# Mixture stage in units of 896 columns, four light experts, one set of PSUM banks

## The reference

```python
logits = x @ w_router;  top_vals, top_idx = top_k(logits, 2);  gates = softmax(top_vals)
for e in range(8):      # combine[e] = gate of e for the tokens that chose e, else 0
    out += combine[e] * ((silu(x @ we_gate[e]) * (x @ we_up[e])) @ we_down[e])
```

## Time and profile before

| | before |
|---|---|
| median of 3 runs, us | 1305.75 |
| profiled execution: its own time, us | 1306.28 |
| profiled execution: span from first to last instruction, us | 1304.5 |
| TensorE matmul busy | 1258.1 us, 96% |
| VectorE busy | 1115.2 us, 85% |
| ScalarE busy | 930.0 us, 71% |
| read from memory | 428.66 MB |
| DMA busy in the 40 slices of the page | 4 to 9 tenths in slices 0 to 11, 9 in slices 12 to 38 |

### The profile page before, as it was taken

How to read it: one execution, slowest core, us unless ns; L and a number is a source line. 1 busy time by engine, 2 the same in 40 slices (tenths; PEclk the granted TensorE clock), 3 DMA queues, 4 the chain that set the end, 5 groups by cost and what they waited for, 6 DMA issues and landing times.

```text
span 1304.5 us, 15757 instructions
## 1 busy us (share of the span) xinstructions
PE 1258.1 (96%) x6233; PEld 1052.4 (81%) x6233; DVE 1115.2 (85%) x873; ACT 930.0 (71%) x734; POOL 47.7 (4%) x57
## 2 busy tenths in 40 slices
PE   9999999999999999999999999999999999999986
PEld 8988888888888888777877887787777788777875
DVE  6987555577989999899899899988999999989897
ACT  5675444454877887888787777878878887878763
POOL 0100000001000000000000000000000000000110
PEclk9999999999999999999999999999999999999998
DMA  9948555546569999999999999999999999999992
GB/s 319 345 144 271 187 190 191 193 139 217 189 222 346 397 398 389 399 397 397 398 397 401 397 400 386 397 398 397 398 401 397 397 397 397 395 397 397 402 397 77
DMA packets 190147, 435.52 MB, mean 334 GB/s; under 512 B 8196, under 2 KB 50228, under 8 KB 175732
## 3 DMA queue, kind: packets, MB, share of 16 engines
q1 hardware_dynamic: 186272, 421.06, 86.5%
q0 software_dynamic: 3712, 13.37, 2.9%
q10 hardware_dynamic: 84, 0.02, 0.0%
HBM read 428.66 MB, written 5.77 MB: 333 GB/s over the span
## 4 chain that ended last, share of the span: by engine, by line
PE 40%; DMA 38%; DVE 13%; ACT 7%; issue 2%; SPq 0%; DVEq 0%; ACTq 0%
DMA raw<-in_we_down 29%; DVE w_lo L978 11%; ACT w_hi L619 7%; DMA raw<-in_we_up 6%; PE turn L1736 4%; PE turn L1733 4%; PE accp L1624 4%; PE accp L1626 4%; PE accp L1625 4%; PE turn L1624 3%; PE turn L1626 3%; PE turn L1625 3%; DMA raw<-in_we_gate 2%; PE turn L1735 2%; PE turn L1734 2%
## 5 line engine op out<-in xcount | busy, mean ns | idle before, releaser
L978 DVE TENSOR_TENSOR w_lo<-raw,w_hi 128x2048 fp32r<-128x2048 f32 (+1 forms) x401 | 905.5, 2267 | 114.9 <-ACT w_hi L619 110.4
L619 ACT CAST w_hi<-raw 128x2048 fp32r<-128x2048 f32 x395 | 755.1, 1914 | 214.8 <-DMA raw<-in_we_up 73.4
L1624 PE MATMUL turn<-w_hi,a_hi 128*128 128x512 f32 x552 | 218.8, 396 | 4.8 <-DVE w_lo L978 4.8
L1626 PE MATMUL turn<-w_hi,a_lo 128*128 128x512 f32 x552 | 215.4, 390 | 0.0
L1625 PE MATMUL turn<-w_lo,a_hi 128*128 128x512 f32 x552 | 215.0, 389 | 0.0
L1991 PE MATMUL turn<-w_hi,t_both 128*128 128x512 f32 x336 | 134.8, 401 | 6.9 <-DVE w_lo L978 6.6
L1992 PE MATMUL turn<-w_lo,t_both 128*128 128x512 f32 x336 | 131.5, 391 | 0.0
L1624 PE MATMUL accp<-w_hi,hT_hi 128*128 128x512 f32 (+1 forms) x284 | 113.0, 398 | 16.0 <-DVE hT_lo L978 16.0
L1624 PEld LDWEIGHTS turn<-w_hi,a_hi 128*128 128x128 f32 x552 | 103.8, 188 | 27.3 <-DVE w_lo L978 6.4
L1626 PEld LDWEIGHTS turn<-w_hi,a_lo 128*128 128x128 f32 x552 | 103.6, 188 | 22.1
L1625 PEld LDWEIGHTS turn<-w_lo,a_hi 128*128 128x128 f32 x552 | 103.8, 188 | 20.5
(11 more groups left out here) (287 smaller groups left out, 1566.5 us busy)
## 6 DMA issues: line engine op xcount, KB each, us to landing
raw<-in_we_gate SPq DMA_DIRECT2D x112, 1024.0 KB, 11.3
raw<-in_we_up SPq DMA_DIRECT2D x112, 1024.0 KB, 11.5
raw<-in_we_down SPq DMA_DIRECT2D x112, 1024.0 KB, 11.4
raw<-in_w_in SPq DMA_DIRECT2D x18, 1024.0 KB, 8.8
raw<-in_w_down SPq DMA_DIRECT2D x11, 1024.0 KB, 5.0
raw<-in_w_gate SPq DMA_DIRECT2D x10, 1024.0 KB, 5.3
raw<-in_w_up SPq DMA_DIRECT2D x10, 1024.0 KB, 5.2
raw<-in_w_out SPq DMA_DIRECT2D x8, 1024.0 KB, 9.4
```

What stands on the lines that cost most here:

```text
L619: nc.scalar.copy(w_hi[:, p % PARTS, :], raw[:, p % RING, :]).then_inc(hi_done, 1)
L978: return nc.vector.tensor_tensor(out, whole, hi.bitcast(f32), ALU.subtract)
L1624: nc.tensor.matmul(to, lh, rh, start=start, stop=False, **group)
L1626: return nc.tensor.matmul(to, ll, rh, start=False, stop=stop, **group)
```

## The change

An expert is cut into 4 units of 896 columns (`WIDE`) instead of 7 steps of 512. A unit has twelve pieces instead of six: four of gate and four of up (2 blocks of rows x 896 columns, 1792 of the 2048 columns of a slot, one run being 896 x 4 = 3584 bytes) and four of down (three with two rows per partition, 8192 bytes a run, and one with a single row, 4096 bytes a run). Gate and up sums of 896 columns lie as 2 x 448 in two banks each, and there is only one set: gate in the first two banks of `turn`, up in the other two. h of the unit before is turned into the gate banks, after the first of the four pieces of up (`amid_up`). Four experts instead of three are light, and the last expert is the fourth light one, whose four units end the order. `VISITS`, `SUM_AT` and the lists of ScalarE and VectorE are moved to fit. The first gate runs its hi x hi pass over all rows first.

```diff
-    N_STEPS = E * STEPS
     E_PIECES = 6 * STEPS
-    LIGHTS = 3
+    QUARTERS = 4
+    WIDE = FF_E // QUARTERS
+    PART = WIDE // 2
+    BLOCKS = WIDE // P
+    N_UNITS = E * QUARTERS
+    U_PIECES = 12
...
-    LIGHTS = 3
+    LIGHTS = 4
...
-    ORDER = "HHH" + "HLHLHHL" * 6 + "HLHLHLH" + "HHHH"
-    assert ORDER.count("H") == HEAVIES * STEPS and ORDER.count("L") == LIGHTS * STEPS
+    ORDER = "HHH" + "LH" * 12 + "H" + "L" * QUARTERS
...
+    FETCHED = (("L", 0), ("H", 1), ("L", 1), ("H", 2), ("L", 2), ("H", 3), LAST_ONE)
+    VISITS = ((1, 0), (3, 1), (8, 2), (10, 3), (13, 4), (16, 5), (20, 6))
...
+    SUM_AT = (1, 2, 4, 6)
+    PICK_AT = 7
...
-        return MOE_AT + (6 * i - 2 if i else 0)
+        return MOE_AT + (U_PIECES * i - 4 if i else 0)
...
+    def blocks_of(half):
+        return range(2 * half, min(2 * half + 2, BLOCKS))
+
+    def filled(p):
+
+        q = p - MOE_AT
+        if q < 0:
+            return PIECE
+        at = q + U_PIECES - MOE_PIECES if q >= MOE_PIECES - 4 else (q - 8) % U_PIECES if q >= 8 else q
+        return 2 * WIDE if at < 8 else len(blocks_of(at - 8)) * D
...
-        def gate_bank(i):
-            return turn[:, 2 * (i % 2), :]
-
-        def up_bank(i):
-            return turn[:, 2 * (i % 2) + 1, :]
+        gate_banks, up_banks = (turn[:, 2 * i:2 * i + 2, 0:PART] for i in range(2))
+        hT_bank = turn[:, 0:2, :].rearrange("p b c -> p (b c)")[:, 0:WIDE]
+        gateT_bank, upT_bank = turn[:, 0, 0:PART], turn[:, 1, 0:PART]
+        sums_bank = turn[:, 1, PART:PART + 4]
+        tokens_bank = turn[:, 2:4, :].rearrange("p b c -> p (b c)")
+        picks_bank = turn[:, 2, 0:TOK]
...
-                dst = raw[:, p % RING, :].rearrange("p (k f) -> p k f", k=src.shape[1])
+                dst = raw[:, p % RING, 0:filled(p)].rearrange("p (k f) -> p k f", k=src.shape[1])
                 sp.dma_start(dst, src).then_inc(slot_filled[p % RING], 16)
...
+                        for pair in range(4):
+                            load(step_at(i) + 4 * j + pair,
+                                 expert_rows(w, ORDER[i], k)[:, 2 * pair:2 * pair + 2, s * WIDE:(s + 1) * WIDE])
                 if i:
                     k, s = expert_step(i - 1)
-                    for half in range(2):
-                        r0 = (2 * s + half) * HALF
-                        load(step_down(i - 1) + half, expert_part(we_down, ORDER[i - 1], k, r0))
+                    for pair in range(4):
+                        r0 = (BLOCKS * s + 2 * pair) * P
+                        load(step_down(i - 1) + pair, expert_part(we_down, ORDER[i - 1], k, r0, len(blocks_of(pair))))
...
             def leave_gate(i):
-                used(step_at(i) + 1)
+                used(step_at(i) + 3)
                 if light(i):
-                    nc.scalar.copy(silu_e[:, i % 2, :], gate_bank(i)).then_inc(few_copied, 1)
+                    nc.scalar.copy(parts(silu_e[:, i % 2, :]), gate_banks).then_inc(few_copied, 1)
                 else:
-                    nc.scalar.activation(silu_e[:, i % 2, :], gate_bank(i), ACT.Silu).then_inc(e_silu, 1)
+                    nc.scalar.activation(parts(silu_e[:, i % 2, :]), gate_banks, ACT.Silu).then_inc(e_silu, 1)
 
             def leave_up(i):
-                used(step_at(i) + 3)
-                nc.scalar.copy(h_e[:, i % 2, :], up_bank(i)).then_inc(few_copied, 1)
+                used(step_at(i) + 7)
+                nc.scalar.copy(parts(h_e[:]), up_banks).then_inc(few_copied, 1)
...
+                if kept_at(i) is not None:
+                    keep_ys(kept_at(i))
+                splits(b + 4, b + 6)
                 leave_gate(i)
                 if i == 0:
+                    splits(b + 7, b + 11)
+                    continue
+                split_hi(b + 7)
+                if light(i - 1):
+                    split_hi(b + 8)
                     silu_few(i - 1)
                     round_few(i - 1)
                 else:
                     round_h(i - 1)
+                    split_hi(b + 8)
+                splits(b + 9, b + 10)
+                if light(i):
+                    leave_up(i)
+                if i in (1, 2):
+                    scale_tokens(i - 1)
+                splits(b + 11, b + 14)
+                after_down(i)
+                if i < N_UNITS - 1:
+                    split_hi(b + 15)
             split_hi(MOE_AT + MOE_PIECES - 1)
...
+                if kept_at(i) is not None and KEPT[kept_at(i)][0] == "L":
+                    fold_ys(kept_at(i))
+                splits(b + 4, b + 7)
                 if i == 0:
+                    split_lo(b + 8)
                 elif light(i - 1):
+                    split_lo(b + 8)
                     times_few(i - 1)
                     rest_of_few(i - 1)
                 else:
                     rest_of_h(i - 1)
+                    split_lo(b + 8)
+                splits(b + 9, b + 10)
                 if not light(i):
                     times_up(i)
                 after_up(i)
+                split_lo(b + 11)
+                if i:
+                    splits(b + 12, b + 14)
+                    if visit_at(i) is not None:
+                        rest_of_tokens(visit_at(i))
+                    if i < N_UNITS - 1:
+                        split_lo(b + 15)
             split_lo(MOE_AT + MOE_PIECES - 1)
...
+            def rows_pair(i, which, pair):
+
+                kind, (e, _) = ORDER[i], expert_step(i)
+                to = (gate_banks, up_banks)[which]
+                wh, wl = wide_rows(split(step_at(i) + 4 * which + pair))
+                for kk in range(2):
+                    k = 2 * pair + kk
+                    for c in range(2):
+                        if kind == "L":
+                            few = xg_few[e % 2][:, k, :]
+                            nc.tensor.matmul(to[:, c, :], few, wh[:, kk, c, :], start=(k == 0), stop=False)
+                            last = nc.tensor.matmul(to[:, c, :], few, wl[:, kk, c, :], start=False, stop=(k == KD - 1))
+                        else:
+                            last = product(to[:, c, :], (xg_hi[e % 2][:, k, :], xg_lo[e % 2][:, k, :]),
+                                           (wh[:, kk, c, :], wl[:, kk, c, :]), k == 0, k == KD - 1)
+                last.then_inc(piece_used, 1)
...
+            def up_left(i):
+
+                if light(i):
+                    pe.wait_ge(few_copied, 2 * number(i))
                 else:
+                    pe.wait_ge(e_h, number(i))
+
+            def gate_left(i):
+
+                if light(i):
+                    pe.wait_ge(few_copied, 2 * number(i) - 1)
+                else:
+                    pe.wait_ge(e_silu, number(i))
 
             def before_up(i):
 
+                up_left(i - 1)
+                if visit_at(i - 1) is not None:
+                    pe.wait_ge(xg_done, visit_at(i - 1) + 1)
+                if i - 1 == PICK_AT:
+                    pe.wait_ge(slots_read, 1)
+
+            def amid_up(i):
+
+                gate_left(i)
                 if i in SUM_AT:
                     sum_tokens(SUM_AT.index(i))
+                turn_h(i - 1)
+
+            def after_down(i):
+
                 if visit_at(i) is not None:
+                    up_left(i)
                     turn_tokens(visit_at(i))
                 if i == PICK_AT:
+                    up_left(i)
+                    transpose_pick(picks_bank, 0).then_inc(slots_written, 1)
...
+            for i in range(N_UNITS):
                 if i == 0:
                     first_gate()
-                elif i < N_STEPS:
-                    bank_read(i - 1)
-                    rows_step(i, 0)
-                if 0 < i < N_STEPS:
-                    turn_h(i - 1)
-                if i < N_STEPS:
+                else:
+                    for pair in range(4):
+                        rows_pair(i, 0, pair)
                     before_up(i)
-                    rows_step(i, 1)
+                for pair in range(4):
+                    if pair == 1 and i:
+                        amid_up(i)
+                    rows_pair(i, 1, pair)
                 if i:
-                    if i < N_STEPS:
-                        down(i - 1)
-                    else:
-                        last_down()
+                    down(i - 1)
+                after_down(i)
+            last_down()
             last_scatter(2)
```

More of the change, by code:

```diff
@@ L54, in hybrid_trunk_kernel @@
     FEW = P // 2
[L55 removed]
+    MOE_PIECES = U_PIECES * N_UNITS
     DENSE_AT = MIX
@@ L2000, in few_half_down @@
                     for c in range(2):
                         cols = slice(c * BANK, (c + 1) * BANK)
-                        nc.tensor.matmul(accp[:, 2 + c, :], left, wh[:, j, cols], start=(first and j == 0), stop=False)
-                        last = nc.tensor.matmul(accp[:, 2 + c, :], left, wl[:, j, cols], start=False,
-                                                stop=(last_one and j == 1))
```

(28 more changed lines are left out.)

323 lines of the change are left out of this document (142 added, 181 removed).

## The result

The changed kernel takes 1317.58 us (median of 4 runs, 1315.30 to 1320.68), the kernel before beside it 1305.91 (1305.45 to 1306.39): ratio 1.0093, interval 1.0081 to 1.0105. It is slower by 0.9%. The forecast was 1279, the range 1266 to 1294. The profiled execution took 1316.43 us with a span of 1314.7, 36.4 us more than the 1278.3 of the sum.

A forecast was written before the change was run, and what follows sets the result against it. Bound taken as DMA bytes per us in the mixture stage: after 455, gate and up 521.0, down 250.3, others 26.0 put the last landing at 1252.3; plus end 24.0, stalls 2 and 1.25 gives 1279, range 1266 to 1294.

The forecast's parts named there:

- the tail: End of the kernel, from last landing to finish: 24.0 us, of which 3.8 before the last down matmuls.
- odd stalls: Waits such as the first token fetch behind down of unit 0: 2 us charged in all.
- still hidden, with little to spare: Mixture stage: VectorE needs 53.4 us per heavy-light pair of units against 55.6 of data; ScalarE about 24 of 27.8 a unit.
- ten pieces of store: Mixture stage: four split and six loaded pieces absorb TensorE's waits of at most 5.5 us a unit, so nothing charged.
- the bubble after a light unit: VectorE idles for one cast (1.6 us) and a rounding (0.5) in a step after a light unit, still hidden.
- the start: Mixture stage up to 455 us: TensorE sets the pace, unit 2 ends at 454.4, 36.5 MB of weights landed.
- more and smaller pieces: Weight loads: 384 transfers instead of 336, costed at nothing because other transfers are in flight behind each.
- The 2 us per transfer: Skill page's own cost of each DMA transfer: 48 more would be 96 us if exposed; the forecast did not charge it.
- The rate: Gate and up loads in runs of 3584 bytes go at 404 GB/s instead of 387, about 408 overall.
- rival C: Slower: TensorE's wait for `leave_gate` is not absorbed; 4 us of stall a unit costs 64 us, 1343; chance 0.08.
- Rival A: VectorE's and ScalarE's lists bind at 28.2 us a unit, 29 units lose 12 us: 1291; chance 0.16.
- a DMA share clearly under 1: Sign in the middle of the mixture stage that the forecast is wrong and rival A or rival C holds.

The follow-up runs named there:

- inter: Changed kernel with, after a light unit, ScalarE's silu and rounding and VectorE's product each moved ahead of a cast or rest: 1327.68 us, ratio 1.0163.
- slots table: Load slots varied in both kernels: changed kernel 1359.34 us with five, 1317.58 six, 1310.25 seven; kernel before 1308.03, 1305.91, 1303.62.

## Why the prediction was wrong

The direction was wrong: I forecast some 27 us less, and it became 12 more. The profiled span is 36.4 us over my sum. 29.9 of them are the last landing (1282.2 instead of 1252.3), 8.5 the tail (32.5 instead of 24.0), and 2 that I had charged for odd stalls go back.

**The step that failed** is the one that made VectorE and ScalarE "still hidden, with little to spare" (53.4 of 55.6 us a pair), together with "ten pieces of store". I compared mean load with mean supply and gave the difference as slack. The terms themselves held: rests back to back are 1.94 us for 1792 columns (16.70 us for eight and one of 1024 columns), and the bubble after a light unit, said to be 2.1 us, is 0.64 + 1.18 = 1.8. (The 683 and 417 ns leave 0.15 us an instruction and not 0.07, which is what the back-to-back 2.21 us leave; the sum used the right one.) What failed is the cover. A slot is refilled only after VectorE's rest, in the order of the list, so 7.6 us in which two rests are done, where the data want more than three, empty the queue. VectorE does catch up within the pair, and the queue fills again, but DMA time already lost doesn't come back: from 736 to 748 some 3.9 MB are moved where 404 GB/s would move 4.85, 2.3 us of data. After the start, which is told below, 21.7 us are lost over 14.5 pairs, 1.5 us a pair. The runs bear it out: slots and a lighter VectorE each bring part of it back and together 25.7 us, a lighter TensorE alone 2.8, less than the runs scatter.

Neither the load nor the store is enough by itself. The kernel before has the same load (704.83 of 770 us, 91.5%; 94% with long runs) and with five slots the same store, and its DMA stays full. What the changed kernel has besides is the coarse list, the single set of banks and the fourth light expert. What isn't settled: the lighter VectorE shortens the bubble's neighbours, the catching up, and each slot's holding time at once. No run took away the bubble alone (`inter` moved it to ScalarE), and none had only one of the three. That the coarse list is the one is argued from the trace of the pair, not shown.

**A slot holds less.** I counted pieces, "more and smaller pieces" at nothing. But six slots held 6 x 1.0486 = 6.3 MB, 16.3 us of data at 387; now mostly 0.9175 each, 5.5 MB, or 13.6 us at 404. The slots table prices that: at six slots the new kernel stands where a slot is worth 42 us on one side and 7 on the other; the old one lies on the flat part (2 and 2), even with five. So fewer bytes cost time only together with the rest of the change. The 2 us per transfer that I quoted stand, in the Trainium skill's "DMA: Bandwidth & Descriptors", under "Anatomy of one DMA — SWDGE (gpsimd) path" and not under "Measured", and my loads are issued by SyncE. No run here changed the number of transfers alone; the 408 GB/s of the middle leave no room for 96 us.

**The start.** I took 36.5 MB as landed by 455. Of the weights' queue this much went by afterwards (DMA, 455 to 1285, to be read beside the earlier trace rows):
```profile
q1 hardware_dynamic: 79244, 319.12, 97.8%
```
352.3 - 319.1 = 33.2 MB, less even than the 35.0 of before. 3.3 MB at 404 are 8 us. TensorE began as said, at 374.3, but it ended unit 2 at 458.4 instead of 454.4, which is half of the 8 us: unit 2 took it 30.4 us instead of 29.6, and units 0 and 1 together 3.5 more than said. From 400 to 460 the share is 0.98 with 366 GB/s. A lighter VectorE leaves that (368; with seven slots 366), a lighter TensorE makes it 379, and both with seven slots 388. So TensorE does take part in the pace of the start, as I had assumed; why fewer pieces than the forty were loaded ahead of it stays open.

**The tail.** I had the silu, the product and the roundings follow the last landing in 3.8 us. From the landing to the first of the last down matmuls it is 10.3. Two casts waited for places in `w_hi` that TensorE held for down, which I had not looked for. After the wait there were two casts and two rests to do, where I had counted one cast and a part of one rest. And eight matmuls ran at the lower clock (0.43 us apart for 3.6 us, instead of 0.23: 1.7 us). The lightened kernels with seven slots have much the same end, 31 us.

**What held.** The rate: 405 where the queue is full, against 404 forecast, and 408 over the middle once the engines allow it. By the rule of the Trainium skill, "DMA: Bandwidth & Descriptors", section "Why small descriptors are slow (HBM only)", an estimate from the 387 of 2 KB was 395. The trace is above that, as it was for 8 KB (423 against 400). That the old kernel is bound by data: 37 us for longer runs. TensorE not the bound: shown by its lightening. No wait of TensorE on `leave_gate` worth the name: its folds and turns wait 4.8 us in all for ScalarE's copy of the gate from 455 to 1278, so rival C's mechanism didn't occur though its sign did. Rival A had the right place and too small a size: it priced a unit at 28.2 us, and units took 28.4, but it left the start and the tail as they were, and gave 1291. Had I added A's 12 us, the start's 8 and the tail's 8.5, I would have had 1308 instead of 1279, with the sign in doubt and 10 us still missing. My own test, "a DMA share clearly under 1", was set too low as well. In the changed kernel the windows from 704 to 728, where data bind, read 1.01 to 1.04, and the window from 736 to 740 reads 0.82; a mean of 1.01 over both hides the gaps.

## What to carry to other kernels

The mean load of an engine that frees the load slots doesn't say whether it is hidden: at 91% it was with the old lists and was not with the new ones. Count the slots in bytes and in us of data, and compare with the longest stretch in which the list frees fewer slots than the data fill, not with the mean. A cheap test is a kernel with one slot less: a slope of 2 us says that there is store to spend, one of 42 that there isn't. It has to be made on the changed kernel. Made on the old one before the change, it gave 2 us and would have let this change pass. And ask for each term that has the data's pace (start, middle, tail) which engine really sets it there.

## What the runs showed of the hardware

- Reading gate and up in runs of 8192 bytes instead of 2048 took the kernel before from 397 to 416 GB/s over 770 us, and from 1305.8 to 1268.33 us.
- Over the middle, the share reads 1.04 in the kernel before, 1.01 in the same kernel with runs of 8192 bytes, and 1.02 in the lightened kernels at 407 to 408 GB/s, though windows of 4 us under 360 GB/s are rare in all of them (2 to 6 of 192). So shares are comparable only between kernels of the same packet sizes.
- After 6.03 us of idle TensorE ran at a granted clock of 0.50 for 3.6 us here: 0.43 us from matmul to matmul instead of 0.23. In the kernels with work taken off TensorE its mean granted clock in the middle was 0.94 to 0.97 instead of 1.00.
